# Up weights of an expert as two transfers of 2 MB, reloaded when all up products are done

## What is computed

```python
for e in range(N_EXPERTS):                       # 32
    hid = jax.nn.silu(t @ w_up1[e]) * (t @ w_up3[e])   # w_up1, w_up3: 1024 x 512 each
    y = y + combine[:, e:e + 1] * (hid @ w_down[e])    # w_down: 512 x 1024
```

## Time and profile before

| | |
|---|---|
| three timed executions | 1183.03 us median (1181.74 to 1185.07) |
| profiled execution | 1180.34 us |
| its span | 1178.2 us |
| TensorE products, share of the span | 88% |
| bytes moved by DMA | 282.69 MB, 240 GB/s over the span |
| of these through SP's queue (q1) | 266.98 MB |

### The profile page before, as it was taken

How to read it: one execution, slowest core, us unless ns; L and a number is a source line. 1 busy time by engine, 2 the same in 40 slices (tenths; PEclk the granted TensorE clock), 3 DMA queues, 4 the chain that set the end, 5 groups by cost and what they waited for, 6 DMA issues and landing times.

```text
span 1178.2 us, 16402 instructions
## 1 busy us (share of the span) xinstructions
PE 1039.5 (88%) x6914; PEld 521.4 (44%) x6914; DVE 348.4 (30%) x593; ACT 256.0 (22%) x403; POOL 171.6 (15%) x222
## 2 busy tenths in 40 slices
PE   3899999999998999999998799997878777877786
PEld 1578644466555676544445433332323222332221
DVE  1332566465448442114226511000000000000004
ACT  2342350076552222232023000000000000000004
POOL 0345100013320100000100111211111111011102
PEclk9599999999999999999999899999999999899998
DMA  8443304443320002335424799999999999999995
GB/s 326 148 139 129 138 6 142 143 143 108 114 100 37 3 4 75 109 113 209 199 104 179 261 383 392 403 406 399 406 403 408 405 412 406 393 399 402 412 413 225
DMA packets 71184, 282.69 MB, mean 240 GB/s; under 512 B 9498, under 2 KB 18988, under 8 KB 46554
## 3 DMA queue, kind: packets, MB, share of 16 engines
q1 hardware_dynamic: 63408, 266.98, 58.6%
q0 software_dynamic: 5120, 8.40, 2.2%
q10 hardware_dynamic: 2602, 6.52, 1.5%
HBM read 277.66 MB, written 12.60 MB: 246 GB/s over the span
## 4 chain that ended last, share of the span: by engine, by line
PE 51%; SPq 29%; DMA 7%; DVE 6%; ACT 4%; issue 2%; POOL 1%; ACTq 0%; POOLq 0%; DVEq 0%
SPq L388 20%; PE ps L1596 7%; SPq L392 5%; PE ps L1477 5%; PE ps L1906 4%; SPq L396 3%; PE ps L1490 2%; PE ps L1607 2%; DMA ring<-in_w_up 2%; PE ps L1491 2%; PE ps L1492 2%; PE ps L1842 2%; PE ps L1852 2%; PE ps L1815 2%; PE ps L1522 2%
## 5 line engine op out<-in xcount | busy, mean ns | idle before, releaser
L1906 PE MATMUL ps<-arena 128*64 128x512 f32 x672 | 151.7, 596 | 33.7 <-DMA arena<-in_w_up 33.7
L1363 DVE TENSOR_TENSOR arena<-arena,ps 128x256 f32<-128x256 f32 x32 | 13.5, 422 | 415.6 <-ACT arena L898 415.6
L1596 PE MATMUL ps<-arena,ring 128*128 128x512 f32 x256 | 118.6, 604 | 0.4 <-DMA ring<-in_w_in 0.4
L1906 PEld LDWEIGHTS ps<-arena 128*64 128x64 f32 x672 | 48.7, 137 | 135.2 <-issue 104.0
L1921 PE MATMUL ps<-arena 128*64 128x512 f32 x336 | 81.8, 631 | 19.7 <-DMA arena<-in_w_down 15.1
L1906 PE MATMUL ps<-ring,arena 128*64 128x512 f32 x352 | 80.3, 597 | 16.2 <-DMA ring<-in_w_up 16.2
L898 ACT ACTIVATE arena<-ps 128x256 f32<-128x256 f32 x32 | 12.3, 383 | 258.9 <-PE ps L1906 258.9
L1596 PEld LDWEIGHTS ps<-arena,ring 128*128 128x128 f32 x256 | 46.1, 190 | 49.2 <-issue 47.2
L905 ACT ACTIVATE arena<-ps 128x512 f32<-128x512 f32 x32 | 19.1, 597 | 187.6 <-PE ps L1921 187.6
L527 POOL TENSOR_SCALAR_AFFINE_SELECT arena<-arena 128x128 f32<-128x128 f32 x64 | 32.4, 540 | 186.3 <-DVE arena L1086 168.6
L1906 PEld LDWEIGHTS ps<-ring,arena 128*64 128x64 f32 x352 | 25.1, 137 | 69.5 <-issue 40.1
(11 more groups left out here) (353 smaller groups left out, 1474.2 us busy)
## 6 DMA issues: line engine op xcount, KB each, us to landing
arena<-in_w_up SPq DMA_DIRECT2D x84, 1024.0 KB, 30.9
ring<-in_w_up SPq DMA_DIRECT2D x44, 1024.0 KB, 28.3
ring<-in_w_down SPq DMA_DIRECT2D x11, 2048.0 KB, 34.8
arena<-in_w_down SPq DMA_DIRECT2D x11, 2048.0 KB, 32.3
ring<-in_w_mod SPq DMA_DIRECT2D x10, 2048.0 KB, 9.1
arena<-in_w_down SPq DMA_DIRECT2D x20, 1024.0 KB
ring<-in_w_in SPq DMA_DIRECT2D x6, 2048.0 KB, 8.5
ring<-in_w_in SPq DMA_DIRECT2D x8, 1024.0 KB, 9.0
```

Of the source, the lines that this page charges most:

```text
L1596: last = mm(ps[:, bank, :], w[:, k, P * (n % 2):P * (n % 2) + P], hT[:, k, :], start=(k == 0), stop=(k == KD - 1))
L1906: last = mm(ps[64 * hf:64 * hf + 64, UP_BANK[u], :].rearrange("p (m n) -> p m n", m=2), hgT[:, k, :], up_pair(u, k)[:, :, 256 * hf:256 * h ...
```

## The change

The parts m = 0 and m = 1 become one. For each of the two up matrices one transfer of 2 MB with one row of 16 KB per partition is issued, on the semaphore `w_in_sem[u][0]`. `up_half` goes; SP waits for `up_done`, and issues both. TensorE waits for both ahead of the first product of an expert. The down weights stay as they are.

```diff
         def load_expert(eng, u, m, e):
 
-            if m < 2:
+            if m == 0:
                 for i in range(2):
-                    src = esrc[i][:, bass.ds(e, 1), 2048 * m:2048 * m + 2048].rearrange("p a n -> p (a n)")
-                    eng.dma_start(eset_up[u][i][:, 2048 * m:2048 * m + 2048], src).then_inc(w_in_sem[u][m], 16)
+                    eng.dma_start(eset_up[u][i], esrc[i][:, bass.ds(e, 1), :].rearrange("p a n -> p (a n)")).then_inc(w_in_sem[u][0], 16)
...
             with sp.Fori(0, LOOPED // NSET - 1) as it:
                 for u in range(NSET):
-                    sp.wait_ge(up_half, NSET * it + (u + 1))
+                    sp.wait_ge(up_done, NSET * it + (u + 1))
                     load_expert(sp, u, 0, NSET * it + (NSET + u))
-                    sp.wait_ge(up_done, NSET * it + (u + 1))
-                    load_expert(sp, u, 1, NSET * it + (NSET + u))
                     sp.wait_ge(down_done, NSET * it + (u + 1))
                     load_expert(sp, u, 2, NSET * it + (NSET + u))
...
                 pe.wait_ge(w_in_sem[u][0], it * 32 + 32)
                 for k in range(KD):
-                    if k == KD // 2:
-                        last.then_inc(up_half, 1)
-                        pe.wait_ge(w_in_sem[u][1], it * 32 + 32)
                     for hf in range(2):
```

More of the change, by code:

```diff
@@ L301, in build @@
             "logit_done", "gsum_ready", "oh_ready", "rank_done", "sel_ready", "idx_done", "route_ready"))
-        w_in_sem = [[sem(f"expert_w{m}_in{u}") for m in range(3)] for u in range(NSET)]
-        up_half = sem("up_half")
+        w_in_sem = [[sem(f"expert_w{m}_in{u}") if m != 1 else None for m in range(3)] for u in range(NSET)]
         hrow_zero, idx_link, dst_link, dst_ready = sem("hrow_zero"), sem("idx_link"), sem("dst_link"), sem("dst_ready")
@@ L445, in _ @@
             load_expert(sp, 1, 0, 1)
-            load_expert(sp, 1, 1, 1)
             sp.wait_ge(y_done, NT)
@@ L450, in _ @@
             load_expert(sp, 0, 0, 0)
-            load_expert(sp, 0, 1, 0)
             sp.wait_ge(logit_done, NT)
@@ L454, in _ @@
             load_expert(sp, 2, 0, 2)
-            load_expert(sp, 2, 1, 2)
             load_expert(sp, 2, 2, 2)
@@ L470, in _ @@
                         e = sp.value_load(nblk_i[0:1, bass.ds(NSET * it + 2 + u, 1)], min_val=0, max_val=E - 1)
-                        sp.wait_ge(up_half, NSET * it + (LOOPED + u + 1 - NSET))
+                        sp.wait_ge(up_done, NSET * it + (LOOPED + u + 1 - NSET))
                         load_expert(sp, u, 0, e)
-                        sp.wait_ge(up_done, NSET * it + (LOOPED + u + 1 - NSET))
-                        load_expert(sp, u, 1, e)
                         sp.wait_ge(down_done, NSET * it + (LOOPED + u + 1 - NSET))
@@ L481, in _ @@
             for u in range(E - LOOPED):
-                sp.wait_ge(up_half, NSET * again + (u + 1))
+                sp.wait_ge(up_done, NSET * again + (u + 1))
                 sp.sem_inc(register_pass, 1)
                 load_expert(sp, u, 0, LOOPED + u)
-                sp.wait_ge(up_done, NSET * again + (u + 1))
-                sp.sem_inc(register_pass, 1)
-                load_expert(sp, u, 1, LOOPED + u)
                 sp.wait_ge(down_done, NSET * again + (u + 1))
```

## The result

| | before | changed |
|---|---|---|
| median of the timed executions | 1181.78 us (7, with the three above) | 1188.57 us (7) |
| range | 1181.22 to 1185.07 | 1187.62 to 1190.92 |
| ratio, 95% interval | | 1.005 [1.0039, 1.0062] |
| profiled execution, its span | 1180.34, 1178.2 us | 1187.62, 1185.5 us |

The time lies in the range of the prediction, and the sign is right; the size is that of its rival B. The 6.8 us are between the medians; by the ratio it is 5.9 us, with an interval of 4.6 to 7.3. In the profiled executions the difference is 7.3 us.

What follows compares the result with a forecast made beforehand. The prediction took one uninterrupted DMA stream of expert weights, with its start, rate and tail, as the bound. 3.3 + 0 - 2.1 + 3.0 = +4.2 us, set on the median 1183.03, gave 1187.2 us, range 1179.5 to 1192.

Steps and rivals of the forecast that it cites:

- rival B: Stream of weights: its rate does not move, so both delays stay, +6.5 us, 1189.5 us; chance 0.20.
- Step 1: Start of the stream: the first refill waits for all 32 up products of expert 0, dry queue 3.3 us longer.
- Step 2: Steady state: one wait for 4 MB instead of two for 2 costs 0, hidden by the stream.
- Step 3: Up weights' stream: rows of 16 KB instead of 8 save 2.1 us over 29 experts, from 0 to 4.3.
- The line a + b x bytes: Cost of a row per DMA engine: a is 9.2 ns, b 37.7 ns per KB.
- Step 4: Tail: all up products of expert 30 run after its weights land, +3.0 us, from 2.4 to 3.4.
- Rival A: Stream of weights: a higher rate pays for both delays, 1185.0 us or less; chance 0.33, 0.10 of it over 0.3% faster.
- rival C: Expert stage: long rows get in the way of gathers and scatters, 14 us over 29 experts, 1202 us; chance 0.05.
- Rival D: TensorE's clock falls behind the one longer wait; only the tail pays, +1.7 to +3.4, 1189 to 1191 us; chance 0.07.

Runs made afterwards that it cites:

- the 8 KB kernel: Changed kernel, but each up matrix goes as two transfers of 1 MB with rows of 8 KB, issued together: 1188.54 us, ratio 1.0067.
- the kernel that is late but at its start: Changed kernel with rows of 8 KB, but the first refill's first half issued at half of expert 0's products as before: 1184.42 us, ratio 1.0025.
- The run with 4 KB: Changed kernel, but each up matrix goes as four transfers of 0.5 MB with rows of 4 KB: 1195.04 us, ratio 1.0121.
- tail whole: Kernel before, but TensorE waits for both halves of experts 30 and 31 ahead of their first product: 1183.84 us, ratio 1.0022.
- waits filled less: Changed kernel with 2 idle calls (1.85 us) behind the down products of each looped expert: 1188.59 us, ratio 1.0063.
- the two fillings: Changed kernel with idle products behind each looped expert's down products, 2 calls or 4: 1188.59 us and 1212.82 us.

## Why the prediction was right or wrong

*What bounds the kernel.* Right. The stream from the first refill to expert 30's up weights took 454.6 us before, and between 453.8 and 455.3 in every profiled kernel with rows of 8 or 16 KB throughout in which TensorE waits for those weights, whatever moved around it; the end moved with its start.

*Step 1, +3.3 us.* The mechanism is shown, by adding it alone (+4.4, or 6.1 by the ratio) and by taking it alone away (-4.1); delaying by 9.0 instead of 3.3 cost 8.2 to 9.2. The size was short by 0.8 us (taken away) to 1.6 (in the profile of the changed kernel). In the changed kernel's profile 1.5 us of the 4.9 are expert 0's products at the lower clock; its second profile and that of the 8 KB kernel show 8.4 and 8.5 us too. But the kernel with the late first refill alone had 7.03 in its profile and also measured over 3.3, within its wide interval. The changed kernel with two idle calls, which is the same up to there, had 7.03 again. So whether these products meet a lower stretch of the clock differs between executions of like code, and how much of the term's excess it is stays open.

*Step 2, 0.* Right, by the kernel that is late but at its start, and by the one wait per expert.

*Step 3, -2.1 us (0 to -4.3).* This is the step that failed. The measured value is 0, the near end of its bounds: 16 against 8 KB is 0.3 us between medians, within the noise. The line a + b x bytes was fitted to rows of 2 and 8 KB and drawn on to 16. The run with 4 KB shows that it bends: below 8 KB a row costs (6.5 us for twice as many, where the line gives 8.5), above it doesn't. The sentence "whatever holds 8 KB rows at 421 may be a limit per byte" was the right one, and the middle between the ends the wrong choice: the stream at 428 to 431 GB/s in its best stretches had little room left.

*Step 4, +3.0 us (2.4 to 3.4).* Right within its bounds: +2.5 in the profile, +2.8 alone, +2.9 with the first refill restored. What holds is its floor of 2.4, the chain through expert 31. In five profiles without halves (the changed kernel twice, 8 KB, tail whole, waits filled less) the first sum starts 28.0 to 28.2 us behind the landing of expert 30, whether its products took 7.09 or 10.08 us and its scatter 6.07 or 2.96. The chain through expert 30 is nearly level with it by an offset that was only half foreseen: its products end 5.0 us later (3.4 by their number, and 1.6 by a clock that this step did not reckon with), and the scatter gives back 2.1.

*Sum and rivals.* 3.3 + 0 + 0 + 3.0 = 6.3 is what is left without step 3, and rival B said 6.5; measured are 6.8. That they agree so well is partly luck: the start cost 0.8 to 1.6 us more than either reckoned with, and the tail 0.5 less in the profile. The forecast time of 1187.2 is luck in another way. It is only 1.4 us below the measured 1188.57, though the difference was 2.6 short, because it was set on a median of three (1183.03) that seven executions put 1.25 lower. The strips were read one slice late (the full stretch begins with slice 23, not 24), and nothing hangs on it. Rival A and rival C are out by the 8 KB kernel. Rival D is half right: the clock fell to 0.93 as its wait suggested, and in steady state the slack held it. In the tail it was hidden where it fell on expert 30, and in the one profile where it fell on expert 31 it cost 1.6 us. That it is the slack that hides this is shown by the two fillings: 1.85 us in each wait cost nothing, 3.6 us cost 24 us.

## What to carry to other kernels

In a stage that is one continuous transfer, look at its two ends: how long the queue is dry before the first buffer comes free, and what is left behind the last landing. Both are paid in full, and what is done between them, waits of 3 us and buffers freed 3.4 us later, is free as long as the stream has a backlog. Before crediting a larger row or transfer, see how near the present rate is to the best stretch of the trace; a price per row fitted on small rows doesn't carry on upward. Splitting finer stops paying where the next wait stands (here the down weights, 5 us behind), and it shortens the rows. At the far end, reckon every chain to the last step: a faster clock for the last expert but one gains nothing where the last one's weights set the end.

## What the runs showed of the hardware

- Rows of 16, 8 and 4 KB in the stream of weights: 404, 404 and 400 GB/s. At the start of a stream rows of 4 KB ran at 301 to 346 GB/s for 4 us, with the engines busy at 0.94 or more.
- A gather beside 16 KB rows took longer than beside 8 and 4 KB, from issue to landing 9.6, 7.2 and 6.4 us, a scatter 8.3, 6.6 and 6.2. It is hidden here, but a kernel that waits for a gather would pay for long rows.
- SP's queue seems to take a number of rows rather than of bytes: with rows of 4 and 8 KB the up weights land 17.9 and 29.0 us after their issue, SP being held back. An estimate from what the queue moved in the 244 us (94.04 and 94.95 MB) has 6.9 and 11.3 MB under way; with the down weights' rows of 8 KB among those of 4 KB, that is about 1400 rows in either. With 16 KB they land after 37 us, and SP waits for buffers instead (224.1 us on the up products where it was 25.9).
- Products that follow a wait for weights can run at the lower clock: 32 of them took 8.66 us behind a wait of 2.27, 10.08 behind one of 6.02, and 7.09 where the waits before had been filled.
- Placing 1.85 us of idle products in each wait of 3 us lifts the mean granted clock from 0.93 to 0.99.
